# A fused conv, dilated-attention and expert-retrieval block: other warm-up products, and one product for each channel sum

## The reference

```python
xn = rmsnorm(x, norm1_g)
x = x + hybrid_mixer(xn, w_in, ...)        # conv branch and 12 attention heads, gated, mixed
hn = rmsnorm(x, norm2_g)
x = x + peer(hn, peer_w_q, sub_keys, u, v) # 16,384 experts, 16 picked for each of 8 heads
```

```python
def rmsnorm(x, g):
    return x * lax.rsqrt(jnp.mean(x * x, axis=-1, keepdims=True) + EPS) * g
def layernorm(x, g, b):
    mu = jnp.mean(x, axis=-1, keepdims=True)
    var = jnp.mean(jnp.square(x - mu), axis=-1, keepdims=True)
    return (x - mu) * lax.rsqrt(var + EPS) * g + b
# conv branch: u = a * sigmoid(gate); 31 taps per channel; silu(layernorm(u)) @ w_proj
# peer: top 16 of product keys, softmax gates, gelu(u_tab[e] . x) * gate, sum of v_tab[e]
```

## Time and profile before

| | |
|---|---|
| median of three runs | 997.36 us (996.97 to 997.46) |
| profiled execution | 997.07 us |
| its span (first to last instruction) | 995.2 us |
| TensorE busy | 989.8 us (99%), 7822 products or passes |
| VectorE, ScalarE, GpSimd busy | 774.9, 506.8, 465.3 us |
| mean transfer rate | 183 GB/s |

### The profile page before, as it was taken

The page is one execution under the profiler, slowest core; times in us unless marked ns, Lnnn a source line. Parts: engine busy times, 40 slices in busy tenths (PEclk is TensorE's granted clock), DMA queues, the critical chain, the costliest instruction groups (busy, mean ns, idle before and its releaser), DMA issues.

```text
span 995.2 us, 21854 instructions
## 1 busy us (share of the span) xinstructions
PE 989.8 (99%) x7822; PEld 917.0 (92%) x7822; DVE 774.9 (78%) x1304; ACT 506.8 (51%) x789; POOL 465.3 (47%) x198
## 2 busy tenths in 40 slices
PE   9999999999999999999999999999999999999998
PEld 9998999999999999999999999888888888888887
DVE  5999784868899996097777777988888876776764
ACT  6663877544555544544444444444444445554443
POOL 3664366656689999874444444100000004344442
PEclk9999999999999999999999999999999999999999
DMA  6684445654455565555555555555554555556562
GB/s 242 211 308 150 149 148 162 212 201 149 150 197 200 171 211 188 191 176 184 177 180 174 182 172 169 185 175 170 177 180 171 182 174 190 190 189 195 186 203 90
DMA packets 52619, 181.95 MB, mean 183 GB/s; under 512 B 5943, under 2 KB 9155, under 8 KB 52452
## 3 DMA queue, kind: packets, MB, share of 16 engines
q1 hardware_dynamic: 52292, 181.16, 54.4%
q10 hardware_dynamic: 288, 0.27, 0.1%
HBM read 180.33 MB, written 3.43 MB: 185 GB/s over the span
## 4 chain that ended last, share of the span: by engine, by line
PE 93%; DVE 5%; ACT 1%; issue 0%; POOL 0%; ACTq 0%; DVEq 0%; POOLq 0%
PE bank L1218 50%; PE bank L1527 35%; DVE bank L798 3%; PE bank L1476 3%; PE bank L1319 1%; PE bank L1233 1%; PE bank L1451 1%; DVE lo L354 1%; PE bank L1242 1%; PE bank L1553 1%; PE bank L1335 1%; ACT hi L335 0%; PE bank L1358 0%; PE bank L1346 0%; PE bank L1249 0%
## 5 line engine op out<-in xcount | busy, mean ns | idle before, releaser
L354 POOL TENSOR_TENSOR lo<-raw,hi 128x1024 fp32r<-128x1024 f32 x184 | 462.4, 2527 | 515.9 <-ACT hi L335 515.4
L335 ACT CAST hi<-raw 128x1024 fp32r<-128x1024 f32 x332 | 348.0, 1049 | 218.0 <-PE bank L1527 186.3
L1218 PE MATMUL bank<-norm_space,hi 128*128 128x256 f32 x2624 | 452.4, 278 | 0.2 <-POOL lo L354 0.2
L1218 PEld LDWEIGHTS bank<-norm_space,hi 128*128 128x128 f32 x2624 | 396.2, 188 | 1.8 <-issue 1.2
L1218 PE MATMUL bank<-norm_space,lo 128*128 128x256 f32 x1312 | 362.8, 277 | 0.0
L1527 PE MATMUL bank<-hi,norm_space 128*128 128x512 f32 x1008 | 273.8, 391 | 0.0
L1218 PEld LDWEIGHTS bank<-norm_space,lo 128*128 128x128 f32 x1312 | 246.4, 188 | 0.0
L1527 PEld LDWEIGHTS bank<-hi,norm_space 128*128 128x128 f32 x1008 | 188.0, 188 | 38.5
L354 DVE TENSOR_TENSOR lo<-raw,hi 128x1024 fp32r<-128x1024 f32 x148 | 189.2, 1279 | 27.4 <-ACT hi L335 27.3
L1527 PE MATMUL bank<-lo,norm_space 128*128 128x512 f32 x504 | 155.5, 390 | 0.0
L1145 DVE TENSOR_TENSOR norm_space<-act,norm_space 128x256 fp32r<-128x256 f32 x128 | 111.7, 876 | 48.8 <-ACT norm_space L665 48.8
(11 more groups left out here) (183 smaller groups left out, 651.5 us busy)
## 6 DMA issues: line engine op xcount, KB each, us to landing
raw<-u_tiles SPq DMA_DIRECT2D x128, 512.0 KB, 3.3
raw<-v_tiles SPq DMA_DIRECT2D x128, 512.0 KB, 3.3
raw<-front SPq DMA_DIRECT2D x76, 512.0 KB, 3.8
toeplitz<-bias_row SPq DMA_DIRECT2D x6, 384.0 KB, 7.5
bias<-toeplitz SPq DMA_DIRECT2D x12, 128.0 KB, 3.5
resid<-x_t SPq DMA_DIRECT2D x2, 512.0 KB, 4.7
qk<-sub_keys SPq DMA_DIRECT2D x1, 1024.0 KB, 8.0
y<-act SPq DMA_DIRECT2D x3, 256.0 KB, 2.0
```

The source lines that it names most:

```text
L335: act_e.copy(hi[:, s, :], raw[:, s, :]).then_inc(hi_ready, 1)
L354: eng.tensor_tensor(lo[:, s, :], raw[:, s, :], hi[:, s, :].bitcast(F32), ALU.subtract)\
L1218: ins = pe.matmul(dst, w_[:, s, u * P:(u + 1) * P], x_[:, k, :], start=first and i == 0 and p_ == 0, stop=last and i == n - 1 and p_ == 2)
```

## The change

- The warm-up has 20 products with ones instead of 27, and behind them 136 products on a part of `norm_space` that VectorE clears at its very start: 8 of 512 columns; 8 of 512 columns whose stationary operand has 66 columns; 8 of 512 columns in float16; 88 of 256 columns, eight for each of eleven distances in memory between the two operands; 8 whose moving operand is read at every second element; 8 read at every 16th; and 8 of 256 columns with 66 stationary columns. They wait for the new semaphore `cleared`. All results are unused.
- For each of the four channel sums VectorE makes one more addition of 128x256, and TensorE one product instead of two.

```diff
-WARM_UP = 27
+WARM_UP = 20
+WARM_EACH = 8
+WARM_APART = (448, 64, 96, 128, 160, 192, 224, 288, 352, 416, 480)
...
+            dve.memset(norm_space[:, 0:6 * T].bitcast(F32), 0.0).then_inc(cleared, 1)
             dve.wait_ge(gain_in, 16)
             for k in range(XG_ACT):
...
             dve.tensor_tensor(sq[:, 0:2, :], sq[:, 0:2, :], part_, ALU.add).then_inc(pair_sums, 1)
+            dve.wait_ge(pair_sums, 3)
+            dve.tensor_tensor(sq[:, 0, :], sq[:, 0, :], sq[:, 1, :], ALU.add).then_inc(pair_sums, 1)
...
                 if n == LNSUM_AT - 1:
                     dve.wait_ge(tap, CB * TAPS)
                     dve.tensor_tensor(sq[:, CB:CB + 2, :], acc[:, 0:2, :], acc[:, 2:4, :], ALU.add).then_inc(acc_pairs, 1)
+                    dve.wait_ge(acc_pairs, 1)
+                    dve.tensor_tensor(sq[:, CB, :], sq[:, CB, :], sq[:, CB + 1, :], ALU.add).then_inc(acc_pairs, 1)
...
                 if n == LNVAR_AT - 2:
                     dve.wait_ge(centred_sq, 1)
                     dve.tensor_tensor(sq[:, CB:CB + 2, :], sq[:, 0:2, :], sq[:, 2:4, :], ALU.add).then_inc(acc_pairs, 1)
+                    dve.wait_ge(acc_pairs, 3)
+                    dve.tensor_tensor(sq[:, CB, :], sq[:, CB, :], sq[:, CB + 1, :], ALU.add).then_inc(acc_pairs, 1)
...
             x_lo(2 * KB - 1)
+            dve.wait_ge(squared, 3 + KB)
+            dve.wait_ge(square_run, KB - 2)
+            dve.tensor_tensor(sq[:, 0, :], sq[:, 0, :], sq[:, KB - 1, :], ALU.add).then_inc(square_run, 1)
...
             for _ in range(WARM_UP):
                 pe.matmul(bank[5][:, 0:P], ones[:, :], ones[:, :], start=True, stop=True)
+            pe.wait_ge(cleared, 1)
+            wide, beside = norm_space[:, 0:2 * T], norm_space[:, 2 * T:2 * T + P]
+            for columns in (P, 66):
+                for _ in range(WARM_EACH):
+                    pe.matmul(bank[5][0:columns, :], beside[:, 0:columns], wide, start=True, stop=True)
+            half, half_beside = wide.bitcast(F16)[:, 0:2 * T], norm_space[:, 2 * T:2 * T + P // 2].bitcast(F16)
+            for _ in range(WARM_EACH):
+                pe.matmul(bank[5][:, :], half_beside, half, start=True, stop=True)
+            for apart in WARM_APART:
+                at = SHIFT + 4 * T - apart // 4
+                for _ in range(WARM_EACH):
+                    pe.matmul(bank[5][:, 0:T], norm_space[:, at:at + P], norm_space[:, SHIFT:SHIFT + T],
+                              start=True, stop=True)
+            stepped = norm_space[:, 0:2 * T].rearrange("p (t a) -> p a t", a=2)[:, 0, :]
+            turned = norm_space[:, 0:T].rearrange("p (t a) -> p a t", a=16)
+            for order in (stepped, turned):
+                for _ in range(WARM_EACH):
+                    pe.matmul(bank[5][:, 0:T], beside, order, start=True, stop=True)
+            at = SHIFT + 4 * T - 112
+            for _ in range(WARM_EACH):
+                pe.matmul(bank[5][0:66, 0:T], norm_space[:, at:at + 66], norm_space[:, SHIFT:SHIFT + T],
+                          start=True, stop=True)
...
                 b = start(("ssq1",))
-                pe.wait_ge(pair_sums, 3)
-                for k in range(2):
-                    ins = pe.matmul(b[:, 0:T], ones[:, :], sq[:, k, :], start=k == 0, stop=k == 1)
-                step(ins)
+                pe.wait_ge(pair_sums, 4)
+                step(pe.matmul(b[:, 0:T], ones[:, :], sq[:, 0, :], start=True, stop=True))
...
             b = start(("ssq2",))
-            pe.wait_ge(square_run, KB - 2)
-            pe.wait_ge(squared, 3 + KB)
-            pe.matmul(b[:, 0:T], ones[:, :], sq[:, 0, :], start=True, stop=False)
-            step(pe.matmul(b[:, 0:T], ones[:, :], sq[:, KB - 1, :], start=False, stop=True))
+            pe.wait_ge(square_run, KB - 1)
+            step(pe.matmul(b[:, 0:T], ones[:, :], sq[:, 0, :], start=True, stop=True))
```

More of the change, by code:

```diff
@@ L276, in hybrid_block @@
         const = sem("const")
+        cleared = sem("cleared")
         squared = sem("squared")
@@ L1390, in _ @@
                     b = start(("lnsum",))
[L1391 to L1394, removed]
+                    pe.wait_ge(acc_pairs, 2)
+                    step(pe.matmul(b[:, 0:T], ones[:, :], sq[:, CB, :], start=True, stop=True))
                 if n == LNVAR_AT:
                     b = start(("lnvar",))
[L1397 to L1400, removed]
+                    pe.wait_ge(acc_pairs, 4)
+                    step(pe.matmul(b[:, 0:T], ones[:, :], sq[:, CB, :], start=True, stop=True))
                 if n == min(TURN_AT):
```

## The result

The changed kernel takes 1015.74 us (median of three, 1015.5 to 1016.28), the kernel before 997.36 us. The ratio is 1.0189, with a 95% interval of 1.0175 to 1.0203: it is 18.4 us slower, where 15.8 us were forecast. The sign and the main cause are as predicted, and 2.6 us are missing. Executions of one kernel differ by 1 to 2 us here (the kernel before took from 996.24 to 997.81 us), so a single pair says no more than that about the total; the lengths of most single rows repeat far better.

The account below looks back on a forecast made before the run. TensorE was taken to bound the kernel: 18.23 us for added products, less 1.56 for the warm-up and 0.86 for the sums, makes +15.8 us, so 1013.2 us. The stated range was 1010.5 to 1018.5, the forecast's own 1012 to 1016.

Parts of the forecast that it names:

- the prediction's own signs of being wrong: A long U or V row with another length, or the 136 products taking under 17 or over 20 us.
- TensorE bounds, so added products are paid in full: Whole kernel: TensorE is busy 99% of the span, with no wait behind the warm-up to hide added products.
- Seven products of ones fewer: Warm-up: 14 passes fewer at 111.6 ns each save 1.56 us.
- The memset is hidden: Start: VectorE's clearing is done at about 3 us, 5 us before TensorE waits for it, and costs nothing.
- The 136 products: Behind the warm-up on TensorE: 5.44 us for 512 columns, 12.70 for 256, 0.09 for a type switch; 18.23 us.
- `ssq1` and `ssq2`: Two channel sums: one TensorE product fewer wins 0.43 us each, VectorE's addition being hidden.
- `lnvar`: Channel sum: VectorE's addition of 0.41 us mostly fills a 0.38 us wait ahead of L354; 0.1 us worse if uncovered.
- The gain of `lnsum` and `lnvar` is lost in a longer wait at the transposes: At L1346: 0.86 us won on two channel sums, 0.86 us lost in TensorE's longer wait.
- Rivals 1 and 2: First: U tiles at 117.8 ns, 6.3 us more, 0.06; second: 312 products and predecessors at 113.4, 2.7 us less, 0.10.
- Rival 3: Products on the cleared array: distance or step makes them dearer by 4.9 + 1.6 us, 1019.7 us; chance 0.08.
- Rival 4: All TensorE products: the warm-up settles a third, faster pace, up to 6.7 ns each, 52 us, giving 961; chance 0.02.
- Rival 5: Start: ones end before the clock rises, or `cleared` comes late; a few us more, at most 1016; chance 0.02.

Follow-up runs that it names:

- e10_after_what: 20 products of ones, then six times 4 float32 products of ones and fp32r packs of 24, 8 and 24 at set operand distances; 1039.69 us in one execution.
- e3_no_steps: The changed kernel with the 16 stepped products reading contiguous columns instead; 1013.88 against 996.97 us for the kernel before, ratio 1.0172.
- e4_sums_psum: The kernel before (27 products of ones) with all four channel sums changed, the pair sums of `lnvar` going through PSUM; 995.9 against 996.96 us, ratio 0.9991.
- after_again: The changed kernel unaltered, measured and profiled a second time; 1015.81 us over five runs against 997.14 for the kernel before, ratio 1.0185.
- e6_turned_late: The kernel before with the 16 transposes of the residual behind the last query tile instead of the third; 997.49 against 996.96 us, ratio 1.0029.

## Why the prediction was right, and where it was not

The direction, the cause and most of the size are as forecast, and 1015.7 us lies within the stated range. But it lies near the upper end of the forecast's own 1012 to 1016, and one of the prediction's own signs of being wrong came true: the 136 products took more than 20 us. The upper end had been reasoned from slower products and steps, which is the larger of the two misses; for the smaller one, at `lnvar`, the text had no term of its size, and only the room left for the products took it in. That part was luck.

- **TensorE bounds, so added products are paid in full.** Right: the first tile starts 18.8 us later and the U tiles 19.05.
- **Seven products of ones fewer, 1.56 us.** Right by the profiled pair, 1.55, with some luck: in both of these executions the passes went over to 112 ns at 6.6 us. In `e10_after_what` the same 40 passes took 6.49 us and not 7.27.
- **The memset is hidden.** Right. It was done by 2.5 us, and TensorE came at 8.2.
- **The 136 products, 18.23 us.** The term was mis-sized: 20.29. The step taken at the low end, "nearest in kind", was the wrong choice for the 16 with a step: both kinds cost the high end of the bounds (225 ns), 1.8 us more, and `e3_no_steps` gave 1.5 us of it back. The text had also let the rule of the Trainium skill spare the step of 2, which these rows show as dear. The 96 with another distance cost the 0.4 us that was given as their near bound.
- **`ssq1` and `ssq2`, 0.43 us each.** Right by their rows: `ssq2` is one row of 0.43 us.
- **`lnvar`.** This step failed. The addition was priced at 0.41 us from a row in which one operand lies in PSUM, and called covered. It took 2.51 us, since GpSimd had three subtractions back to back beside it and both operands lay in SBUF. The row that could have warned was in the prediction's own list: L354 on VectorE, 2.97 us in the earlier trace rows, for an operation that takes 1.22 elsewhere.
- **The gain of `lnsum` and `lnvar` is lost in a longer wait at the transposes.** Wrong in place and cause. The wait at L1346 before was for ScalarE's square root of `lnvar`, which moves with TensorE. Nothing of it grew. The sums lose most of their gain at `attend`, through the long addition, and with that taken away in `e4_sums_psum` about 1 us of gain is there. Another 0.4 us goes one tile ahead of `lnvar`: TensorE, early by then, waits for GpSimd's low part, and two products start 0.50 us apart (149.47 and 149.97) that were 0.12 apart before. Between the first tile and the U tiles the profile has +0.3 us where -0.86 was forecast, and +0.1 in `after_again`.
- **Rivals 1 and 2, another pace in a long row.** Neither came true for its long row. On a small scale rival 1 did: 240 products of the front ran at 117.8 ns in the first profiled execution of the changed kernel and at 113.3 in the second, and the wait behind them took up most of that 1.0 us. `e4_sums_psum`, with the old warm-up, has them at 117.8 as well, so the odd products are not what decides. And rival 1's full size is real: `e6_turned_late` has it in the profiled execution, with 6.4 us against the 6.3 worked out, and by their times in four more of twelve. The ground given against it, that the jobs between are the same as before, is no protection, since executions of one program differ by just this length.
- **Rival 3, distance or step is dear.** Half true: the step is, at 1.8 us; the distance is not, at 0.4.
- **Rival 4, a third pace that pays the warm-up back.** Not seen: no pack of 256 fp32r columns went below 113 ns, and the long rows kept their length.
- **Rival 5, the clock or `cleared` late.** Not seen in the profiled execution: the passes ran at 112 ns from 6.6 us on, and TensorE did not wait for `cleared`.

By the profiled pair the misses are 2.1 us in the products, 1.2 us between the first tile and the U tiles (about 1.0 in the sums and at most 0.2 from the slower stretch) and 0.2 us in the first U tiles beside the gates, 3.5 us together (19.3 against 15.8). The medians moved by 18.4; the 0.9 us between the two is within the scatter of executions.

## What to carry to other kernels

Where TensorE bounds a kernel as it does this one, expect warm-up products beyond what raises the clock to be paid one for one; here they left nothing behind. Before a short VectorE instruction is called hidden, look at what GpSimd does beside it: with two operands in SBUF it may last as long as GpSimd's instruction, and a reduce that reads from PSUM avoided that here. Keep the moving operand's columns adjacent, at most two float16 apart, and expect a long row of products to have one of two paces, not always the same in two executions of one program: a difference of a microsecond or of six can be that alone.

## What the hardware showed

- VectorE's addition of two SBUF operands, 128x256: 0.42 us with GpSimd idle, 2.51 and 2.52 us beside GpSimd's subtractions; as a reduce of 512 columns from PSUM 0.69 us beside them. A subtraction of 128x1024: 1.22 us beside transfers of 300 GB/s with GpSimd idle, 3.19 us beside GpSimd alone.
- 256 fp32r columns: 113.3 or 117.8 ns at operand distances that are odd multiples of 64 bytes (64, 192, 320 and 448 were tried), 117 to 120 ns at the other distances tried; 218 to 233 ns at steps of 2, 4, 8 and 16. A row of 1440 took 163.29 or 169.66 us.
- 256 float16 columns at steps of 1, 2, 4, 8 and 16: 111, 114, 227, 452 and 460 ns.
- 66 stationary columns save nothing: 118.8 ns for 256 columns, 227.5 for 512, as with 128.
- The same 54 warm-up passes (213 ns apart at the clock's lower level, 112 at the upper) were followed by the first tile at 8.99 to 10.09 us, as the rise came earlier or later in the execution.
